# Masks of sparse attention that multiply by the negative factor, with both halves' factors copied at once

## The reference

```python
q = rms_norm(q); k = rms_norm(k)                 # per head, 64 values
s = einsum('bqhd,bqkd->bqhk', q, k) * scale      # DSA, and NSA's selected and window keys
s = where(ok, s, -1e30)
p = softmax(s, axis=-1)
o = einsum('bqhk,bqkd->bqhd', p, v)              # NSA: times a gate per token and head
```

## Time and profile before

| | |
|---|---|
| median of 3 runs | 2777.93 us |
| profiled execution: time, span | 2784.97 us, 2783.2 us |
| busy in it: TensorE, VectorE, ScalarE, GpSimd | 2647.9, 1639.7, 1146.7, 121.6 us |
| DSA pairs, 1402 to 1486 us: TensorE, VectorE, ScalarE busy | 68.3, 58.5, 62.8 us of 84; granted clock 0.90, DMA share 0.03 |
| NSA pairs, 1654 to 1812 us: TensorE, VectorE, ScalarE busy | 136.7, 123.5, 122.1 us of 158; granted clock 0.96, DMA share 0.02 |

### The profile page before, as it was taken

The page is one execution under the profiler, slowest core; times in us unless marked ns, Lnnn a source line. Parts: engine busy times, 40 slices in busy tenths (PEclk is TensorE's granted clock), DMA queues, the critical chain, the costliest instruction groups (busy, mean ns, idle before and its releaser), DMA issues.

```text
span 2783.2 us, 38256 instructions
## 1 busy us (share of the span) xinstructions
PE 2647.9 (95%) x13607; PEld 2122.7 (76%) x13607; DVE 1639.7 (59%) x3082; ACT 1146.7 (41%) x1990; POOL 121.6 (4%) x106
## 2 busy tenths in 40 slices
PE   7999999999999999999989989899999989999998
PEld 5567888888887788888856865577777768788887
DVE  6235725547876843637874278756677675473452
ACT  4444322226674322225474338722455562322221
POOL 0000000000000000001310010000111110000000
PEclk9999999999999999999999999999999999999999
DMA  4112332321222233323201210022222213323231
GB/s 144 46 47 75 100 105 91 98 91 61 82 77 80 72 106 94 102 84 99 76 24 47 98 39 1 16 76 83 76 69 69 74 48 103 132 91 98 91 104 62
DMA packets 59683, 217.80 MB, mean 78 GB/s; under 512 B 6432, under 2 KB 6560, under 8 KB 59424
## 3 DMA queue, kind: packets, MB, share of 16 engines
q1 hardware_dynamic: 57920, 209.76, 23.9%
q0 software_dynamic: 1632, 6.29, 0.7%
HBM read 211.83 MB, written 4.19 MB: 78 GB/s over the span
## 4 chain that ended last, share of the span: by engine, by line
PE 75%; DVE 14%; DVEq 4%; issue 3%; ACT 3%; ACTq 0%; DMA 0%; POOL 0%; SPq 0%
PE ps L385 22%; PE ps L386 21%; PE ps L387 21%; DVE work L2124 2%; PE ps L526 1%; DVE ring_lo L325 1%; DVE big L3362 1%; DVEq L3420 1%; DVE big L2124 1%; PE ps L777 1%; DVE work L2144 1%; DVE work L2476 1%; DVEq L2479 1%; ACT ring_hi L318 1%; PE ps L587 1%
## 5 line engine op out<-in xcount | busy, mean ns | idle before, releaser
L385 PE MATMUL ps<-a_hi,ring_hi 128*128 128x512 f32 (+1 forms) x1896 | 750.6, 396 | 32.7 <-DVE ring_lo L325 19.0
L387 PE MATMUL ps<-a_hi,ring_lo 128*128 128x512 f32 (+1 forms) x1912 | 741.9, 388 | 0.0
L325 DVE TENSOR_TENSOR ring_lo<-ring,ring_hi 128x1024 fp32r<-128x1024 f32 x356 | 435.4, 1225 | 482.1 <-ACT ring_hi L318 451.4
L386 PE MATMUL ps<-a_lo,ring_hi 128*128 128x512 f32 (+1 forms) x1832 | 712.1, 389 | 0.0
L318 ACT ACTIVATE ring_hi<-ring 128x1024 fp32r<-128x1024 f32 x376 | 395.5, 1055 | 502.9 <-PE ps L387 502.8
L385 PEld LDWEIGHTS ps<-a_hi,ring_hi 128*128 128x128 f32 x1896 | 358.6, 189 | 119.3 <-DVE ring_lo L325 17.9
L387 PEld LDWEIGHTS ps<-a_hi,ring_lo 128*128 128x128 f32 x1912 | 361.8, 189 | 74.4
L386 PEld LDWEIGHTS ps<-a_lo,ring_hi 128*128 128x128 f32 x1832 | 346.4, 189 | 68.4 <-issue 1.0
L386 PE MATMUL ps<-hid_lo,ring_hi 128*128 128x512 f32 (+1 forms) x992 | 380.0, 383 | 0.0
L385 PE MATMUL ps<-hid_hi,ring_hi 128*128 128x512 f32 (+1 forms) x928 | 354.8, 382 | 0.0
L387 PE MATMUL ps<-hid_hi,ring_lo 128*128 128x512 f32 (+1 forms) x928 | 354.4, 382 | 0.0
(11 more groups left out here) (456 smaller groups left out, 3304.1 us busy)
## 6 DMA issues: line engine op xcount, KB each, us to landing
ring<-weights SPq DMA_DIRECT2D x392, 512.0 KB, 3.5
h<-x SPq DMA_DIRECT2D x1, 2048.0 KB, 9.2
residual<-h POOLq DMA_DIRECT2D x4, 512.0 KB, 3.5
h<-residual POOLq DMA_DIRECT2D x1, 2048.0 KB, 11.0
out<-h POOLq DMA_DIRECT2D x1, 2048.0 KB, 7.9
tab<-tables SPq DMA_DIRECT2D x1, 1648.0 KB, 15.4
big<-positions SPq DMA_DIRECT2D x1, 256.0 KB, 3.3
col<-columns SPq DMA_DIRECT2D x1, 164.5 KB, 3.9
```

The costliest lines, as they stand in the source:

```text
L325: dve.tensor_tensor(lo, M.ring[:, b % RING, :], hi.bitcast(F32), ALU.subtract).then_inc(M.sem("blocks_split"), 1)
L385: pe.matmul(out, w_hi, hi, start=start, stop=False)
L386: pe.matmul(out, w_hi, lo, start=False, stop=False)
L387: return pe.matmul(out, w_lo, hi, start=False, stop=stop)
```

## The change

`mask` now multiplies by the negative factor and keeps the minimum, straight into `V.ntop`; the instruction that changed the sign goes, and the drain signals `masked`. `exp` takes -1 as its scale, so it computes exp(-p' + ntop) with p' the negated scores. The negative factors are made once for each mixer, in `M.root`, by one tensor_scalar of 72 (DSA) or 88 columns (NSA) behind the reciprocal; in DSA with a drain in front. The copy of factors takes both halves (two times 4 columns) and stands only in the mask of half 0, with its drain, the wait for the scores and the memset; half 1 has none of them.

```diff
--- before.py
+++ after.py
@@ -1955,10 +1955,11 @@
 
         return self.items[n % len(self.items)]
 
-    def factors(self, M, i, u, half):
-
-        at = i * (QT * self.unroll) + head_column(self.norms, self.first + u, half)
-        return M.inv[:, at:at + QT] if isinstance(at, int) else M.inv[:, bass.ds(at, QT)]
+    def factors(self, M, i, u):
+
+        at = i * (QT * self.unroll) + QT * (self.first + u)
+        rows = M.root[:, 0:8 * self.norms].rearrange("p (h y) -> p h y", h=2)
+        return rows[:, :, at:at + QT] if isinstance(at, int) else rows[:, :, bass.ds(at, QT)]
 
     def stage_pool(self, pool, M, ready, all_ready, more_ready=None):
 
@@ -2073,7 +2074,7 @@
             act.wait_ge(M.sem(f"{A}_masked"), i * (2 * per) + (2 * n + half + 1))
             for t in range(QT):
                 s = V.p[x][:, CAUSAL_AT[t]:CAUSAL_AT[t] + S_LEN[t]]
-                e = act.activation(s, s, ACT.Exp, bias=V.ntop[:, x, t:t + 1], scale=1.0, accum_out=V.sum[:, x, t:t + 1])
+                e = act.activation(s, s, ACT.Exp, bias=V.ntop[:, x, t:t + 1], scale=-1.0, accum_out=V.sum[:, x, t:t + 1])
             e.then_inc(M.sem(f"{A}_exp"), 1)
 
         def keep(i, n, half):
@@ -2115,19 +2116,18 @@
         def mask(i, n, half):
             u, kind = self.item(n)
             m, x = self.kinds[kind][2](half), 2 * (n % 2) + half
-            dve.tensor_copy(V.inv[:, x, :], self.factors(M, i, u + n // per * self.unroll, half))
-            dve.drain()
-            dve.wait_ge(M.sem(f"{A}_scores"), i * per + (n + 1))
-            dve.memset(V.sum[:, x, :], 0.0)
+            if half == 0:
+                dve.tensor_copy(V.inv[:, x:x + 2, :], self.factors(M, i, u + n // per * self.unroll))
+                dve.drain()
+                dve.wait_ge(M.sem(f"{A}_scores"), i * per + (n + 1))
+                dve.memset(V.sum[:, x, :], 0.0)
             for t in range(QT):
                 at = PAIR_S_AT[half][t]
                 dve.tensor_tensor_reduce(V.p[x][:, CAUSAL_AT[t]:CAUSAL_AT[t] + S_LEN[t]], M.ps[:, at:at + S_LEN[t]],
                                          m[:, CAUSAL_AT[t]:CAUSAL_AT[t] + S_LEN[t]],
-                                         V.inv[:, x, t:t + 1], -3.0e38,
-                                         ALU.add, ALU.max, V.top[:, x, t:t + 1])
-            dve.drain()
-            dve.tensor_scalar(V.ntop[:, x, :], V.top[:, x, :], -1.0, None, ALU.mult)\
-               .then_inc(M.sem(f"{A}_masked"), 1)
+                                         V.inv[:, x, t:t + 1], 3.0e38,
+                                         ALU.add, ALU.min, V.ntop[:, x, t:t + 1])
+            dve.drain().then_inc(M.sem(f"{A}_masked"), 1)
 
         def divide(i, n, half):
             u, kind = self.item(n)
@@ -2469,6 +2469,8 @@
             if i + 1 == QT and r == 0:
                 dve.wait_ge(M.sem("norm_root"), 1 + M.past("dsa_norm", "root"))
                 dve.reciprocal(M.inv[:, 0:72], M.root[:, 0:72]).then_inc(M.sem("norm_inverse"), 1)
+                dve.drain()
+                dve.tensor_scalar(M.root[:, 0:72], M.inv[:, 0:72], -1.0, None, ALU.mult)
             if i + 1 == QT and r == TOPK // 16:
                 dve.wait_ge(M.sem("norm_spread"), 1 + M.past("dsa_norm", "spread"))
                 dve.scalar_tensor_tensor(out=R.key, in0=R.key, scalar=R.gain, in1=M.bank(7),
@@ -2834,6 +2836,7 @@
     dve.wait_ge(M.sem("norm_root"), 1 + M.past("nsa_norm", "root"))
     dve.reciprocal(M.inv[:, 0:88], M.root[:, 0:88]).then_inc(M.sem("norm_inverse"), 1)
     dve.drain()
+    dve.tensor_scalar(M.root[:, 0:88], M.inv[:, 0:88], -1.0, None, ALU.mult)
     scaled(0)
     scaled(1)
     rest(2)
```

## The result

| | before | after |
|---|---|---|
| median, beside each other on one chip (5 runs each) | 2778.92 us (2777.47 to 2782.49) | 2765.01 us (2763.80 to 2766.42) |
| ratio | | 0.9945, 95% interval 0.9931 to 0.9959 |
| profiled execution: time, span | 2784.97, 2783.2 us | 2766.42, 2764.6 us |
| mean granted clock of TensorE in it | 0.986 | 0.991 |

The gain is 13.9 us between these medians (interval by the ratio 11.4 to 19.2 us). The prediction said 7.75 us, 2770.2, with a range down to 2765.5. Direction right, size wrong.

The account below looks back on a forecast made before the run. TensorE carries 75% and VectorE 14% of the chain that ended last, mostly VectorE in the changed stretches. Gains 9.07 less 0.27 added, 0.45 ScalarE and 0.6 clock gave 7.75 us: 2770.2 us, range 2765.5 to 2775.0.

Parts of the forecast that it names:

- the clock term: TensorE's granted clock early in both stages: work brought forward may run at the low clock; -0.6 us of the gain.
- (a): VectorE after half 0's masks: without the sign operation the next division's reciprocal starts 0.08 us earlier per step.
- (b): VectorE between divisions and half 1's masks: the mask takes the copy's place, 0.30 us per step, at least 0.22.
- (c): After half 1's masks: a drain instead of the sign releases TensorE, 0.28 us per step, at least 0.17.
- The ScalarE term: ScalarE copying out the first turned piece after scores has 0.09 us too little in five NSA steps: -0.45.
- Its two first steps: DSA's first two steps: TensorE idle only 0.59 and 0.36 us, so gains of 0.42 + 0.19 = 0.61.
- NSA at the turns of GpSimd's loop: Two NSA steps where GpSimd's staged copy limits when queries can be taken: 2 x 0.32 = 0.64 us gained.
- Steps with the branch: NSA steps with the compressed branch's 16 extra matmuls: five of seven gain nothing, two with late masks 0.40 + 0.16.
- Selection: DSA's selection: added drain and tensor_scalar of 72 columns behind the reciprocal cost 0.27 us; nothing in NSA.
- Rival 1: VectorE is all: small gaps on other engines shrink too, gain 14.7 us, 2763.2; chance 0.13 for it or most of it.
- rival 2: Ties cost more: small ends of (b) and (c), clock takes 1.2; gain 5.45, 2772.5; chance 0.21 (gain under 5.6).
- Rival 3: Mask instructions: keeping a minimum costs 0.08 us more each, 192 times, 15.4 us, giving 2785.6; chance 0.04.

Follow-up runs that it names:

- 9: Changed kernel with filler matmuls (compute nothing used) in three TensorE idle times per stage: 2761.4 us median, mean clock 0.9932.
- 10: Kernel before with filler matmuls in the same three TensorE idle times per stage: 2770.1 us median, mean clock 0.9934.
- 2: Changed kernel with one filler matmul less (5 for 6) between a stage's first and second scores: 2770.0 us median against 2765.0.
- 1: Kernel before with one filler matmul more (7 for 6) between a stage's first and second scores: 2780.9 us median.
- 3: Kernel before with 13 filler matmuls for 6 between a stage's first and second scores: 2778.7 us median.
- 4: Changed kernel with 12 filler matmuls for 6 between a stage's first and second scores: 2765.7 us median.
- experiment 8: Changed kernel without the added drain and multiplication by -1 in DSA's selection: 2766.5 us median, 2766.3 at equal clock.

## Why the prediction was wrong, point by point

**Where it failed: the clock term.** The step is "The clock: ... I take -0.6." It asked only whether the low stretch ends at the same moment as before or moves with the work, so it could take back part of a lead and never add to one. But the low stretches stand behind TensorE's long idle times, and the change shortens those. Ahead of the second scores 3.83 became 3.31 us in DSA and 1.97 became 1.44 in NSA; ahead of the last turns 2.18 became 1.46 (DSA) and 2.31 became 1.94 (NSA), all in matmul rows of the two profiles. The mean clock of the runs went from 0.9886 to 0.9910. At 1.92 us per 0.001 that is a gain of 4.7 us (before rounding), with the other sign and nearly eight times the size. The means of the runs differ by 14.3 us (2779.4 and 2765.0), 9.6 at equal clock and 4.7 by clock; the medians by 13.6 to 13.9. That this part comes from the gaps of the two stages is shown by experiments 9 and 10, and 2 agrees. How it is shared among the gaps is not shown: 1, 3 and 4, which changed one gap of each stage, moved the clock less than expected or not at all. The Trainium skill (TensorE: Matmul & The Clock Gate, Part 1) says that the clock is set by how busy the engine has recently been. The runs agree in direction: with the gaps filled with matmuls that compute nothing, the granted clock of both stages was 1.00.

**The profile's offset.** I took the profiled execution as 7 us above the median in both kernels. Before's had a clock of 0.986, among the lowest of its runs; the changed kernel's had 0.991, like all its runs, and is 1.4 above its median. Runs near the median of the kernel before have 0.989; by the slope the 0.003 between give some 6 of the 7 us. So the offset was mostly clock and not a property of profiling.

**The edits: 8.35 summed (9.07 - 0.27 - 0.45), 9.65 measured at full clock.** By itself this would have put the time at 2768.3 (2777.9 - 9.6), inside the range: of the forecast's miss of some 6.5 us, 5.3 are the clock term and 1.3 the edits. By terms:
- (a), reciprocal 0.08 earlier: 0.04 in DSA and nothing in NSA. In DSA it started 0.24 behind the start of the last read (the row here and 1451.72 in the earlier trace rows) and starts 0.20 behind it now:

```profile
1451.48 0.08 DVE L2124 DVE_READ_ACCUMULATOR2_ANT work<- 128x1 f32 x1
```

  In NSA it started 0.27 behind it before (first fence) and does so after (second):

```profile
1703.05 0.08 DVE L2124 DVE_READ_ACCUMULATOR2_ANT work<- 128x1 f32 x1
1703.21 0.17 DVE L2129 TENSOR_SCALAR work<-work 128x4 f32<-128x4 f32 x1
1703.32 0.18 DVE L2136 RECIPROCAL work<-work 128x4 f32<-128x4 f32 x1
...
1707.32 0.08 DVE L2124 DVE_READ_ACCUMULATOR2_ANT work<- 128x1 f32 x1
```

```profile
1691.53 0.08 DVE L2126 DVE_READ_ACCUMULATOR2_ANT work<- 128x1 f32 x1
1691.80 0.18 DVE L2136 RECIPROCAL work<-work 128x4 f32<-128x4 f32 x1 [0.19 <-issue]
...
1695.49 0.08 DVE L2126 DVE_READ_ACCUMULATOR2_ANT work<- 128x1 f32 x1
```

  So the reciprocal does not come forward by what the sign took; what holds it there was not isolated.
- (b), 0.30: right, by the overlap of 0.08 that the row had shown. The Trainium skill (VectorE: DVE Perf Modes, section "The DRAIN you can't avoid"), which I had quoted for the other side, goes on to say that a next instruction which is not held starts earlier; the trace agrees, with the 0.08.
- (c): the release is 0.08 behind the last read, as the earlier trace rows had it (in NSA the read starts at 1695.49, takes 0.08, and scores start at 1695.65), but in NSA it was 0.31 before (1707.71 in the earlier trace rows, less 1707.40), not DSA's 0.36: 0.23 gained, not 0.28. So VectorE gives 0.53 per NSA step, not 0.66. The ScalarE term (-0.45 for five steps) had set the step to 0.57; ScalarE is not what holds the step, since TensorE's idle time ahead of scores ends with VectorE's drain. Two errors that nearly cancel: that the forecast of these steps came out near is luck.
- DSA's steady steps, 0.54 each: 0.54 to 0.56 measured. Its two first steps: 0.57 each at full clock, not 0.42 and 0.19. Their idle times in the earlier trace rows, 0.59 and 0.36, were small because TensorE ran partly at half speed; in the kernel before with the gaps filled they are 0.93 and 0.77. 0.5 us missed.

```profile
1417.70 0.76 PEld L2011 LDWEIGHTS ps<-big,work 64*128 64x128 f32 x7 [0.93 <-issue]
...
1426.42 0.76 PEld L2011 LDWEIGHTS ps<-big,work 64*128 64x128 f32 x7 [0.77 <-issue]
```

- NSA at the turns of GpSimd's loop, 0.32 each: 0.54 and 0.58 at full clock, 0.5 us missed. I took the copy at 1706.63 for one that the scores at 1707.71 wait for. It is the copy for the next pair, whose scores start at 1726.09. In the changed kernel the same copy runs from 1695.12 to 1695.74, and the scores start at 1695.65, before it has ended:

```profile
1695.12 0.62 POOL L1974 COPY work<-big 128x512 f32 x1 [0.79 <-issue]
```

- NSA's five other steps without the branch, 0.57 each after the ScalarE term: 0.53 to 0.57 in four of them, but 0.93 in the last (9.30 to 8.37 us). Why the last gives more is open; it is another 0.3 us missed.
- Steps with the branch: as forecast, 8.96 to 9.05 us; within 0.03 of before in the five that had little more than 0.17 idle, and 0.41 and 0.16 shorter in the two with late masks.
- First double masks, 0.67 each: 0.52 and 0.53. Last turn, 0.46: 0.38. Selection, -0.27: nothing that could be told (experiment 8).

**The rivals.** Rival 1 named 2763.2, the nearest number, by a wrong mechanism: its test was that steps with the branch shrink too, and those that had 0.17 idle did not. That a time falls near a rival's number says nothing for its mechanism. Of rival 2's small ends, (a) and (c) went its way, (b) did not, and the clock went the other way. Rival 3 is out: the minimum takes as long as the maximum, 0.35 us for 128 columns and a read of 0.08.

**What would have shown it blind.** In the profile before, the low stretches of both stages stood behind idle times of TensorE of 1.6 to 3.8 us, and DSA's first two steps stood 4.4 us above two steady ones (21.84 against 17.42). That was the price of the clock there, and the idle time in front of it was one that the change shortens. It belonged in the sum as an upside and at least in the range.

## What to carry to other kernels

Find each stretch of low granted clock, and look at the idle time of TensorE right in front of it: an edit that shortens this idle time can win the stretch back, and an edit that lengthens it loses one; put both into the range. Before comparing two kernels whose times differ by less than a percent, set their runs against the mean clock of each run, and compare at equal clock. And a small idle time in front of an engine that runs slow says nothing on what it could take at full speed. Before a copy is taken as a bound, look up which instruction waits for it: one that ends shortly before another starts need not be what that one waits for.

## What the runs showed of the hardware

- Counted over the profiles of all 13 kernels, without the start of the program: of TensorE's idle times of 1.2 to 2 us, 22 of 204 had a mean clock under 0.85 in the 5 us that followed; of 2 to 2.5 us, 58 of 93; of 2.5 to 4 us, 29 of 34; of over 4 us, 25 of 25. The same gap of one kernel's code can go either way: 3.31 us in the changed kernel was followed by 1.00, and 3.30 and 3.31 in two of its variants by 0.66 and 0.67. So in these profiles it is a chance that grows with the length, and a single profile shows one draw of it.
- Filler matmuls in idle times can be worth about as much as work removed: in three gaps of each stage they took 8.6 us off the kernel before, where the edits take 9.6 at equal clock. 12 more in one gap of 6.55 us came with another 5.9 us, of which an unknown part is the fillers'.
- A drain of VectorE that carries the signal releases TensorE 0.08 us behind the end of the last accumulator read in NSA, where drain and sign took 0.31. But the reciprocal that comes next on VectorE starts no earlier there than it did behind drain and sign together (0.27 us behind the start of that read in both kernels).
- The instruction that keeps a minimum takes as long as the one that keeps a maximum: 0.35 us for 128 columns to 0.75 for 512, with a read of 0.08 behind it.
